# Two transformer blocks on one core: last layer norm reordered, last attention chunks normed by pairs, two pieces of VectorE work moved

## The reference

```
mod = silu(c) @ ada_w + ada_b                      # six rows of 1024 for each layer
for i in (0, 1):
    h = x * (1 + scale1) + shift1
    y = moba_attention(h) if i == 0 else diff_attention(h)
    x = layer_norm(alpha * x + (1 + gate1) * y, ln_g[i, 0], ln_b[i, 0])
    h = x * (1 + scale2) + shift2
    y = square(relu(h @ w_up)) @ w_down
    x = layer_norm(alpha * x + (1 + gate2) * y, ln_g[i, 1], ln_b[i, 1])

# diff_attention, 8 heads, causal, two softmaxes for each head
w = softmax(q1 @ k1.T) - lam * softmax(q2 @ k2.T)
o = w @ v                                           # 256 x 128 for each head
o = rms_norm(o, subln_g) * (1 - lambda_init)        # over the head's 128 columns
y = concat(o) @ w_out
```

## Time and profile before

| | |
|---|---|
| Median of 3 runs | 1258.6 us (1258.38 to 1259.3) |
| The profiled execution | 1259.41 us, its span 1257.6 us |
| PE busy | 1226.0 us (97%) |
| DVE busy | 926.2 us (74%) |
| ACT busy | 615.3 us (49%) |
| Mean granted clock of PE | 0.994 |
| Differential attention, from slot 0 to the next stage's entry | about 950 to 1064 |
| Last stage's last layer norm | 1236.3 to the end |

### The profile page before, as it was taken

One profiled execution on the slowest core, in us unless ns is written; L12 is line 12 of the kernel. 1 busy time (PEld: TensorE's weight loads), 2 busy tenths in 40 slices (PEclk: granted clock), 3 DMA queues, 4 the chain that ended last, 5 costly groups with the idle time before them and its releaser, 6 DMA issues.

```text
span 1257.6 us, 14731 instructions
## 1 busy us (share of the span) xinstructions
PE 1226.0 (97%) x5821; PEld 1007.1 (80%) x5821; DVE 926.2 (74%) x1326; ACT 615.3 (49%) x812; POOL 95.2 (8%) x136
## 2 busy tenths in 40 slices
PE   7999999999999999999999999999999998999996
PEld 5888887888888878888887778888887767888885
DVE  6889869866456789888784568897779687655446
ACT  7344446545664454433556546343455754635240
POOL 2010222002500010000010000000000000000000
PEclk9999999999999999999999999999999999999998
DMA  9999995535445589888465346788744532465630
GB/s 307 342 322 323 313 287 202 189 135 169 159 159 168 177 304 338 311 308 284 156 218 190 114 153 247 285 299 285 274 167 167 191 128 101 168 232 187 199 134 34
DMA packets 132916, 274.31 MB, mean 218 GB/s; under 512 B 6240, under 2 KB 51504, under 8 KB 132848
## 3 DMA queue, kind: packets, MB, share of 16 engines
q1 hardware_dynamic: 114992, 209.80, 48.7%
q0 software_dynamic: 17792, 63.56, 14.7%
q10 hardware_dynamic: 64, 0.02, 0.0%
HBM read 270.41 MB, written 2.93 MB: 217 GB/s over the span
## 4 chain that ended last, share of the span: by engine, by line
PE 87%; DVE 8%; ACT 3%; issue 1%; DMA 1%; SPq 1%; DVEq 0%; ACTq 0%
PE ps L468 26%; PE ps L470 26%; PE ps L469 26%; PE ps L591 3%; DVE lo_w L1374 3%; ACT hi_w L982 1%; DMA w_raw<-in_ffn_w_in 1%; ACT aux L1005 1%; PE ps L731 1%; PE ps L858 1%; PE ps L718 1%; PE ps L755 1%; PE ps L545 1%; PE ps L871 1%; PE ps L843 0%
## 5 line engine op out<-in xcount | busy, mean ns | idle before, releaser
L1374 DVE TENSOR_TENSOR lo_w<-w_raw,hi_w 128x2048 fp32r<-128x2048 f32 x197 | 447.4, 2290 | 83.8 <-ACT hi_w L982 83.6
L468 PE MATMUL ps<-hi_w,xT_hi 128*128 128x512 f32 x1120 | 448.1, 400 | 7.1 <-DVE xT_lo L1396 3.4
L470 PE MATMUL ps<-lo_w,xT_hi 128*128 128x512 f32 x1120 | 437.8, 391 | 0.0
L469 PE MATMUL ps<-hi_w,xT_lo 128*128 128x512 f32 x1120 | 436.7, 390 | 0.0
L982 ACT ACTIVATE hi_w<-w_raw 128x2048 fp32r<-128x2048 f32 x197 | 373.2, 1917 | 44.5 <-DMA w_raw<-in_w_mix_out 12.0
L468 PEld LDWEIGHTS ps<-hi_w,xT_hi 128*128 128x128 f32 x1120 | 210.9, 188 | 56.5 <-issue 10.9
L470 PEld LDWEIGHTS ps<-lo_w,xT_hi 128*128 128x128 f32 x1120 | 210.4, 188 | 45.6
L469 PEld LDWEIGHTS ps<-hi_w,xT_lo 128*128 128x128 f32 x1120 | 211.0, 188 | 40.9
L468 PE MATMUL ps<-hi_w,hT_hi 128*128 128x512 f32 x464 | 181.9, 392 | 0.4 <-DVE hT_lo L1572 0.4
L470 PE MATMUL ps<-lo_w,hT_hi 128*128 128x512 f32 x464 | 180.7, 389 | 0.0
L469 PE MATMUL ps<-hi_w,hT_lo 128*128 128x512 f32 x464 | 180.6, 389 | 0.0
(11 more groups left out here) (236 smaller groups left out, 897.8 us busy)
## 6 DMA issues: line engine op xcount, KB each, us to landing
w_raw<-in_ffn_w_in SPq DMA_DIRECT2D x86, 512.0 KB
aux<-in_ada_w POOLq DMA_DIRECT2D x34, 1024.0 KB, 6.6
w_raw<-in_mlp_w_up SPq DMA_DIRECT2D x32, 1024.0 KB
w_raw<-in_mlp_w_down SPq DMA_DIRECT2D x32, 1024.0 KB
w_raw<-in_w_mix_in SPq DMA_DIRECT2D x26, 1024.0 KB
w_raw<-in_ffn_w_out SPq DMA_DIRECT2D x22, 1024.0 KB
area<-in_ada_w POOLq DMA_DIRECT2D x14, 1024.0 KB, 7.6
w_raw<-in_moba_w_in SPq DMA_DIRECT2D x12, 1024.0 KB
```

The lines of the kernel that those rows point to most:

```text
L468: pe.matmul(dst, lhs_hi, rhs_hi, start=start, stop=False)
L469: pe.matmul(dst, lhs_lo, rhs_hi, start=False, stop=False)
L470: return pe.matmul(dst, lhs_hi, rhs_lo, start=False, stop=stop)
L1374: vec.tensor_tensor(lo_w[:, ring_slot(u), :], w_raw[:, ring_slot(u), :], hi_w[:, ring_slot(u), :].bitcast(F32), ALU.subtract).then_inc(w_l ...
```

## The change

Four pieces are joined.

1. `x_update` takes one tile. In differential attention tile 0 is updated in slot 2 as before, tile 1 in slot 6, between the scores and the combination of head 0.
2. The split of slot 11 moves behind the low parts of pair 1, in slot 12.
3. Chunks 4 and 5, then 6 and 7, are normed by themselves. The sum of squares goes to ACT, which takes the root (`norm_root_of`); DVE takes its reciprocal and one Newton step (`last_rstd`), then multiplies (`last_norm`). Pair 2's transposes and the first six matmuls of the last quarter stand ahead of pair 3's transposes. The 18 matmuls that nobody reads become 6. The table of the square root is asked for ahead of head 6's squares.
4. `finish` takes the root from ACT and does the passes of a tile's second half behind the next quarter's statistics.

```diff
@@ constants @@
-ROOTED = (S_MOBA, S_MLP1, S_DIFF)
+ROOTED = (S_MOBA, S_MLP1, S_DIFF, S_MLP2)
-PAIR_BANK, NORMED = (4, 5, 0, 1), (1, 2, 3, 3)
+PAIR_BANK, NORMED = (4, 5, 0, 1), (1, 2, 3, 4)
@@ PE, slot 14 @@
                         if diff:
-                            busy(0, 18)
+                            busy(0, 6)
                             outputs_T(2)
-                            outputs_T(3)
                         pe.wait_ge(w_lo, u0 + 15)
                         last_quarter(0, 0, 0)
-                        if not diff:
-                            outputs_T(3)
+                        outputs_T(3)
@@ ACT @@
+                def norm_root_of(n):
+
+                    act.wait_ge(norm_in, n + 1)
+                    act.activation(head_root[:, n, :], head_sq[:, 2 * n:2 * n + 2, :].rearrange("p c t -> p (c t)"),
+                                   ACT.Sqrt, scale=1.0 / P).then_inc(norm_root, 1)
...
                 if diff:
+                    act.activation(table_in[:, 3:4], table_in[:, 0:1], ACT.Sqrt)
                     squares(6)
                     weights_out(7)
+                    norm_root_of(0)
                     squares(7)
+                    norm_root_of(1)
                     pair_his(2)
                     pair_his(3)
                     split_hi(u0 + 18)
-                    act.activation(table_in[:, 3:4], table_in[:, 0:1], ACT.Sqrt)
...
             mlp(U_MLP2, B_MLP2)
+            for t in range(NT):
+                root_of(S_MLP2, t)
@@ DVE, the last layer norm @@
             def finish():
+
+                def centred(t, h):
+
+                    z = zt[:, t, half_cols(h)]
+                    steps.inc(vec.scalar_tensor_tensor(out=z, in0=z, scalar=moments[:, t, 0:1], in1=row_g[:, half_cols(h)],
+                                                       op0=ALU.subtract, op1=ALU.mult))
+
+                def shifted(t, h):
+
+                    steps.wait(vec)
+                    vec.scalar_tensor_tensor(out=x[:, t, half_cols(h)], in0=zt[:, t, half_cols(h)], scalar=rstd[:, t:t + 1],
+                                             in1=row_b[:, half_cols(h)], op0=ALU.mult, op1=ALU.add).then_inc(x_fin, 1)
 
                 for t in range(NT):
-                    for h in range(2):
-                        ln_part(S_MLP2, t, h)
-                    ln_finish(t)
-                    for h in range(2):
...
+                    ln_part(S_MLP2, t, 0)
+                    if t == 1:
+                        centred(0, 1)
+                        shifted(0, 1)
+                    ln_part(S_MLP2, t, 1)
+                    ln_variance(S_MLP2, t)
+                    centred(t, 0)
+                    ln_rstd(S_MLP2, t)
+                    shifted(t, 0)
+                centred(1, 1)
+                shifted(1, 1)
@@ DVE, attention @@
+                def last_sums(n):
+
+                    vec.wait_ge(at_sq, 2 * n + 6)
+                    squares = head_sq[:, 2 * n:2 * n + 2, :]
+                    vec.tensor_tensor(squares, squares, head_eps[:, 2 * n:2 * n + 2, :], ALU.add).then_inc(norm_in, 1)
+
+                def last_rstd(n):
...
+                    then(vec.reciprocal(y, head_root[:, n, :]))
+                    then(vec.tensor_tensor(h, y, y, ALU.mult))
+                    then(vec.scalar_tensor_tensor(out=h, in0=h, scalar=-0.5 / P, in1=sums, op0=ALU.mult, op1=ALU.mult))
+                    then(vec.scalar_tensor_tensor(out=head_rstd[:, 0:2 * NT], in0=h, scalar=1.5, in1=y, op0=ALU.add,
+                                                  op1=ALU.mult))
...
                     for event in before:
                         if event[0] == "T":
                             pair_los(int(event[1:]))
+                    if diff and slot == 12:
+                        split_lo(u0 + 11 + AHEAD)
                     for event in before:
                         if event[0] == "S":
                             scores(int(event[1:]))
+                    if diff and slot == 6:
+                        x_update(S_MLP1, 1)
...
-                    split_lo(u0 + slot + AHEAD)
+                    if not diff or slot != 11:
+                        split_lo(u0 + slot + AHEAD)
                     if slot == 2 and diff:
-                        x_update(S_MLP1)
+                        x_update(S_MLP1, 0)
...
                     outputs(6)
+                    last_sums(0)
+                    last_rstd(0)
+                    last_norm(0)
                     outputs(7)
-                    norms(4, 4)
+                    last_sums(1)
+                    last_rstd(1)
                     pair_los(2)
+                    last_norm(1)
                     pair_los(3)
                     split_lo(u0 + 18)
```

More of the change, by code:

```diff
@@ L209, in two_blocks_kernel @@
         head_eps = sb("head_eps", [P, 4, NT])
+        head_root = sb("head_root", [P, 2, 2 * NT])
         shift = sb("shift", [P, NT])
@@ L289, in two_blocks_kernel @@
         xT_pair, xT_lo_pair = sem("xT_pair"), sem("xT_lo_pair")
+        norm_in, norm_root = sem("norm_in"), sem("norm_root")
         chunksT = sem("chunksT")
@@ L1546, in after_ln, with x_update @@
                 split_lo(next_unit + 3)
-            def x_update(s):
-                for t in range(NT):
[L1551 to L1557, removed]
-                    for h in range(2):
-                        ln_part(S_MLP2, t, h)
-                    ln_finish(t)
-                    for h in range(2):
[L1562 to L1565, removed]
-                                                 in1=row_b[:, half_cols(h)], op0=ALU.mult, op1=ALU.add).then_inc(x_fin, 1)
+            def x_update(s, t):
+                vec.wait_ge(z_quarter, quarter(s - S_MOBA, t, 1))
+                then(vec.tensor_tensor(x[:, t, :], zt[:, t, :], row_g, ALU.mult))
+                vec.tensor_tensor(x[:, t, :], x[:, t, :], row_b, ALU.add).then_inc(x_new, 1)
@@ new lines, in finish @@
+            def finish():
+                def centred(t, h):
[6 more added lines that the diff above has]
+                                             in1=row_b[:, half_cols(h)], op0=ALU.mult, op1=ALU.add).then_inc(x_fin, 1)
+                for t in range(NT):
+                    ln_part(S_MLP2, t, 0)
[9 more added lines that the diff above has]
+                shifted(1, 1)
@@ L1677, in mlp @@
                     if i == 1:
-                        x_update(s_before)
+                        for t in range(NT):
+                            x_update(s_before, t)
                     split_lo(u + LEAD + 3)
@@ L1957, in norms, with last_norm @@
                     vec.tensor_tensor(heads, heads, factor.broadcast_to([P, NT, n, P]), ALU.mult).then_inc(at_norm, 1)
+                def last_sums(n):
[3 more added lines that the diff above has]
+                def last_rstd(n):
+                    sums = head_sq[:, 2 * n:2 * n + 2, :].rearrange("p c t -> p (c t)")
+                    y, h = newton[:, 2, 0:2 * NT], newton[:, 3, 0:2 * NT]
+                    vec.wait_ge(norm_in, n + 1)
+                    vec.wait_ge(norm_root, n + 1)
+                    vec.wait_ge(at_norm, 2 + n)
+                    then(vec.reciprocal(y, head_root[:, n, :]))
[3 more added lines that the diff above has]
+                                                  op1=ALU.mult))
+                def last_norm(n):
+                    c = 2 * n + 4
+                    vec.wait_ge(at_out, ab + c + 2)
+                    heads = o2[:, :, c * P:(c + 2) * P].rearrange("p t (c n) -> p t c n", c=2)
+                    factor = head_rstd[:, 0:2 * NT].rearrange("p (c t) -> p t c", t=NT).unsqueeze(3)
+                    vec.tensor_tensor(heads, heads, factor.broadcast_to([P, NT, 2, P]), ALU.mult).then_inc(at_norm, 1)
                 def outputs(c):
```

## The result

The changed kernel takes 1251.71 us (median of 4 runs, 1251.23 to 1252.19) against 1258.95 us (1258.38 to 1259.65) for the kernel before, measured beside it: ratio 0.9942, 95% interval 0.9925 to 0.9959. That is 7.2 us faster, where 7.9 were forecast, and 1.0 us above the predicted time. The profiled executions differ by more: span 1249.4 us against 1257.6.

The account below looks back on a forecast made before the run. PE, busy 97% of the span, bounds the kernel, so time is won at its idle stretches, low clock, or where others finish behind it. 4.0 + 1.9 + 0 + 2.0 = 7.9 us gives 1250.7 us, range 1249.2 to 1253.0.

Parts of the forecast that it names:

- Part 1: Early differential attention: moving half the x update saves 2.4 us of PE idle time and 1.6 us of low clock, 4.0 us.
- (b): Rival: clock falls after slot 3 all the same or elsewhere before slot 12; first part gives 2.4 us; 1252.3 us, chance 0.1.
- (c): Rival: slot 6's half update delays head 0's weights, or weights' DMA holds ACT; 1253 to 1255 us, chance 0.1.
- Part 2: Slot 12: low parts of pair 1 ahead of the split remove PE's idle time there, 1.9 us.
- Part 3: End of attention: norming the last chunks by pairs gains 0, between -1.5 and +1.2 us, as a clock fall eats the gain.
- of 3.2 us on PE 0.8 us reach the norm: End of attention: PE goes on 3.2 us earlier, but DVE's split of unit 18, waiting for ACT, lets the norm gain 0.8 us.
- I take it that the clock falls: At the norm: PE idles 2.0 then 1.1 us, so its clock falls and the next stage loses about 0.8 us.
- (a): Rival: clock does not fall in the norm, chunk norming by pairs keeps 0.8 us or more; 1249.2 to 1249.9 us, chance 0.2.
- (d): Rival: the table load stalls ACT longer than 1.28 us, squares and norm 1.5 us later; 1252.2 us, chance 0.05.
- (e): Rival: with twelve filling matmuls gone, the clock that fell at 1042.1 does not come back; 1266 us, chance 0.02.
- Part 4: Last layer norm: last quarter starts 0.9 us earlier, shorter instruction chain 1.0 us, passes 0.1 us; 2.0 us in all.
- the median of the runs is 1258.6, 0.8 us lower: Base of the predicted time: the kernel before's median, 0.8 us below its profiled execution of 1259.41 us, giving 1250.7 us.

Follow-up runs that it names:

- e2: Changed kernel with both halves of the update of x in slot 2 again: 1254.47 us, ratio 0.9966 to the kernel before.
- e3: Changed kernel with the split of slot 11 ahead of pair 1's low parts again: 1253.93 us, ratio 0.9964 to the kernel before.
- e6: Changed kernel with ACT making unit 18's high part between those of pairs 2 and 3: 1249.15 us, ratio 0.9924 to the kernel before.
- e9: e4 with unit 18's high part ahead of both pairs' on ACT: 1250.94 us, ratio 0.993 to the kernel before.
- e4: Changed kernel with last four chunks normed together, eighteen filling matmuls and table load behind the last split, as before: 1250.63 us, ratio 0.9935 to the kernel before.
- e1: The changed kernel run again with nothing edited: 1251.33 us, ratio 0.9939 to the kernel before.
- e8: Changed kernel with the last layer norm as before: 1252.94 us, ratio 0.9954 to the kernel before.
- e11: The changed kernel run a third time with nothing edited: 1251.98 us, ratio 0.9936 to the kernel before.
- e10: e6 with twelve empty DVE instructions ahead of the last layer norm: 1249.56 us, ratio 0.9917 to the kernel before.
- e5: Changed kernel with nine pairs of unread matmuls in PE's idle stretch ahead of the norm's transposes: 1250.65 us, ratio 0.9936 to the kernel before.
- e7: e6 with two filling matmuls ahead of the norm's transposes and five behind: 1249.54 us, ratio 0.9924 to the kernel before.

## Why the prediction was right, point by point

**Part 1, 4.0 us: right** in both of its terms. 2.29 us of idle time went, the clock stayed up, 4.01 us were measured and the trace of e2 gives them back (the medians, 3.1). Slot 6 took the other half for nothing. Rivals (b) and (c) fell with it: there is no fall of the clock and no new idle stretch between slots 3 and 12.

**Part 2, 1.9 us: right** (2.03, and e3 gives 2.0 back).

**Part 3, nothing: the mechanism right, the sizes off, the sum near by luck.** The bound named, DVE's split of unit 18 behind ACT's activation of it, was the bound: e6 takes it away and e9 shows that it does nothing where PE is the bound. The step "of 3.2 us on PE 0.8 us reach the norm" has 4.1 us on PE (15.33 us from head 7's scores to the restart before, 11.25 now) and 1.68 us at the norm. The forecast had taken head 7's outputs and the six filling matmuls (0.28 us each) at the lower clock of the trace before; the outputs now took 0.75 us in place of 1.44, and the six took 1.34 us. Behind the restart the steps fit: I had 6.8 us from there to the norm, and there are 6.80. 0.7 us of the gain are not the change's: in e4, with the old code, the clock did not fall at head 7's outputs either. By itself, against e4, the part gives 3.35 us on PE and 0.96 us at the norm. PE's idle stretch was 1.56 us where I worked out 2.0. The step "I take it that the clock falls" holds in four of the six traces with these idle stretches (after, e1, e2, e3; not e8 and e11), and costs 1.3 to 1.6 us where I took 0.8. So the norm's gain was 0.9 us over the forecast and the entry's loss 0.5 us over it; that they cancel in part, and leave the sum near nothing, is luck. Rival (a) is therefore no other mechanism but the rest of the executions: e11's profiled one took 1250.05 us, 0.15 above the upper end of the time given for it. With the fall the part gives 0.42 us against the trace before, and loses 0.3 to 0.6 us against e4.

The table load cost its 1.28 us and no more: the next activation started 1.29 us behind its start, and head 6's squares right behind that (6.03 us behind head 7's scores, where it was 5.73: the 0.3 us of the forecast). Rival (d), by which the drain of about 1.38 us in the Trainium skill's "ScalarE: Activation LUTs", section "What ACT_TABLE_LOAD costs", would have come on top, has nothing for it in this trace.

Rival (e), the clock that stays down for the rest of attention, did not come: six filling matmuls and 1.37 us of idle time behind pair 2's transposes left it at 1.00. Each of the eight falls that the thirteen traces show between the start and the last layer norm lasted about 3.4 us.

**Part 4, 2.0 us: the mechanism right, the size off by 0.36.** The last quarter begins 16.19 - 5.31 = 10.88 us into the tail in e10 and in the changed kernel (1229.65 to 1240.53), so the order of the passes gives what it should (before it was 11.82: 0.94 us, forecast 0.9). Behind it I forecast 5.3 us to the last instruction's start; e10 has 5.31, and the changed kernel 5.66, because of the stall ahead of L1575 (0.36 us more than the same step takes on the first tile). That is the mis-sized step: the price of the short chain was right, and on it lies a stall that the rows of before don't show.

**The sum.** 4.01 + 2.03 + 0.42 + 1.64 = 8.10 us by the traces, against 7.9; part 3's surplus and part 4's shortfall offset each other, which is luck again. The medians give 7.2 to 8.0 in the three pairs measured. The predicted time is 0.6 to 1.3 us below the three medians of the changed kernel. A part of that lies in the base, "the median of the runs is 1258.6, 0.8 us lower": beside the changed kernel the kernel before measured 1258.95, and 1259.29 and 1259.44 in the groups of e1 and e11. That is 0.35 of the 1.0 us in the main measurement, where the rest is the smaller gain (7.2 against 7.9), all of the 0.6 us in e1's group, and 0.8 of the 1.3 us in e11's.

## What to carry to other kernels

An idle stretch of TensorE that lies on the path costs what it lasts (2.29 us in slot 4) and, if the clock falls behind it, up to 1.7 us more; one that is off the path costs nothing itself (the entry takes 29.10 us with 1.56 us of idle time in e11 and 29.11 with 0.41 in e6), but the fall behind it cost 1.3 to 1.6 us all the same. So a piece of VectorE work that is moved out of such a place into a wait can bring nearly double its length. When one engine is brought forward, look at once for the instruction of another that stands between it and its consumer: norms by pairs brought PE 3 us forward and gained under 1 us until ACT's activation of one weight unit was moved too. Two edits of which each is worth little alone can be worth 2 us together, and undoing one of them alone does not show that.

## What the runs showed of the hardware that was not expected

- **The same idle stretches, with and without a fall of the clock.** 1.6 and 1.07 us, with the norm's transposes between them: down to 0.50 in four traces, 1.00 in two. 0.42 and 1.07 us: once up (e6), once down (e10). The idle 2.28 us of slot 4 was followed by a fall both times that it was seen (before and e2), the 1.70 us of slot 12 in neither of the two. What decides between them stays open; in all traces without idle time ahead of the norm's transposes (before, e4, e5, e7, e9) the clock stayed up, which is five traces and no proof. The Trainium skill, "TensorE: Matmul & The Clock Gate", section "HAM oscillation", describes waits that bring the clock down again and again; in the profile after it happened once between the start of differential attention and the last layer norm.
- **A stall that belongs to a place in the program.** The 0.46 us between two dependent DVE instructions stood in every profiled kernel with the new last layer norm except e4, e9 and e10, in which the number of DVE instructions ahead of it differs. What makes it is open.
- **A cost of 1.28 us for the table load**, in its old place (1052.24) as in its new one (1033.54), with the next activation 1.29 us behind its start in both.
